# Moving four tiles of the second modulation from the second feed-forward's second down projection to the first mixer's output projection

## The reference, cut to what matters

```python
# first block, second half
x = x + mod[:, 1, 2][:, None, :] * y                 # y = ... einsum('bsd,de->bse', merged, w_out)
h = modulate(x, norm_w[l, 2], mod[:, 2, 0], mod[:, 2, 1])
x = x + 0.5 * mod[:, 2, 2][:, None, :] * swiglu(h, ffn_w13[l, 1], ffn_w2[l, 1])
# second block: modulation vectors, independent of x
mod = (jax.nn.silu(c) @ ada_w[i] + ada_b[i])[:, None, :]              # ada_w: 1024 x 6144
mod_c = (jax.nn.silu(c_ctx) @ ada_w[i][:, :n_ctx_mod] + ada_b[i][:n_ctx_mod])[None, None, :]
```

## Time and profile before

| | |
|---|---|
| median of 3 runs | 1704.6 us (1704.57 to 1707.57) |
| the profiled execution | 1707.38 us, its span 1705.6 us |
| PE busy | 1681.9 us, 99% of the span |
| DVE busy | 1145.5 us, 67% |
| ACT busy | 690.2 us, 40% |
| POOL busy | 67.4 us, 4% |
| transfers | 218.59 MB, mean 128 GB/s |
| mean granted clock of TensorE | 0.997 |

### The profile page before, as it was taken

One profiled execution on the slowest core, in us unless ns is written; L12 is line 12 of the kernel. 1 busy time (PEld: TensorE's weight loads), 2 busy tenths in 40 slices (PEclk: granted clock), 3 DMA queues, 4 the chain that ended last, 5 costly groups with the idle time before them and its releaser, 6 DMA issues.

```text
span 1705.6 us, 24579 instructions
## 1 busy us (share of the span) xinstructions
PE 1681.9 (99%) x8956; PEld 1408.0 (83%) x8956; DVE 1145.5 (67%) x2122; ACT 690.2 (40%) x1048; POOL 67.4 (4%) x56
## 2 busy tenths in 40 slices
PE   7999999999999999999999999999999999999998
PEld 5788888888878868897888888888868988989897
DVE  3778578655655686469969973469675558656563
ACT  4421222234236573354222334342466443626262
POOL 0000000011000000200000000200000200000002
PEclk9999999999999999999999999999999999999999
DMA  9866567332523302537666642354200232434231
GB/s 330 259 203 197 178 201 212 108 103 54 145 74 98 99 1 75 171 106 219 188 205 188 175 116 80 112 169 113 87 1 15 86 112 74 119 85 124 85 108 50
DMA packets 355674, 218.59 MB, mean 128 GB/s; under 512 B 8544, under 2 KB 353668, under 8 KB 355588
## 3 DMA queue, kind: packets, MB, share of 16 engines
q1 hardware_dynamic: 355356, 217.37, 43.8%
q10 hardware_dynamic: 232, 0.09, 0.0%
HBM read 215.34 MB, written 2.11 MB: 127 GB/s over the span
## 4 chain that ended last, share of the span: by engine, by line
PE 95%; DVE 2%; DMA 1%; issue 1%; ACT 0%; SPq 0%; POOL 0%; DVEq 0%; ACTq 0%; POOLq 0%
PE bank L777 24%; PE bank L779 24%; PE bank L778 24%; PE bank L1314 2%; PE bank L1315 2%; PE bank L1313 2%; PE bank L1039 2%; PE bank L1023 1%; PE bank L955 1%; PE bank L959 1%; PE bank L956 1%; PE bank L1101 1%; PE bank L1273 1%; PE bank L1075 1%; DMA GBUF<-in_w_ada 1%
## 5 line engine op out<-in xcount | busy, mean ns | idle before, releaser
L1471 ACT ACTIVATE W_HI<-RAW 128x1024 fp32r<-128x1024 f32 x278 | 292.3, 1056 | 463.2 <-PE bank L779 401.5
L777 PE MATMUL bank<-H_HI,W_HI 128*128 128x512 f32 x1090 | 426.1, 391 | 3.9 <-DVE W_LO L1955 3.8
L778 PE MATMUL bank<-H_LO,W_HI 128*128 128x512 f32 x1090 | 424.7, 390 | 0.0
L779 PE MATMUL bank<-H_HI,W_LO 128*128 128x512 f32 x1090 | 424.7, 390 | 0.0
L1955 DVE TENSOR_TENSOR W_LO<-RAW,W_HI 128x1024 fp32r<-128x1024 f32 x254 | 311.3, 1226 | 95.3 <-ACT W_HI L1471 92.1
L777 PE MATMUL bank<-A_HI,W_HI 128*128 128x512 f32 x714 | 279.7, 392 | 0.0
L778 PE MATMUL bank<-A_LO,W_HI 128*128 128x512 f32 x714 | 278.2, 390 | 0.0
L779 PE MATMUL bank<-A_HI,W_LO 128*128 128x512 f32 x714 | 278.2, 390 | 0.0
L777 PEld LDWEIGHTS bank<-H_HI,W_HI 128*128 128x128 f32 x1090 | 204.7, 188 | 49.3 <-issue 5.1
L779 PEld LDWEIGHTS bank<-H_HI,W_LO 128*128 128x128 f32 x1090 | 204.7, 188 | 42.4
L778 PEld LDWEIGHTS bank<-H_LO,W_HI 128*128 128x128 f32 x1090 | 204.8, 188 | 42.2 <-issue 0.2
(11 more groups left out here) (435 smaller groups left out, 2313.5 us busy)
## 6 DMA issues: line engine op xcount, KB each, us to landing
RAW<-in_ffn_w SPq DMA_DIRECT2D x116, 512.0 KB, 4.8
GBUF<-in_w_ada SPq DMA_DIRECT2D x32, 1024.0 KB, 7.4
RAW<-in_mlp_w SPq DMA_DIRECT2D x64, 512.0 KB, 4.1
RAW<-in_w_in SPq DMA_DIRECT2D x57, 512.0 KB, 3.9
GBUF<-in_ada_w SPq DMA_DIRECT2D x24, 1024.0 KB, 7.2
RAW<-in_w_out SPq DMA_DIRECT2D x16, 512.0 KB, 4.0
RAW<-in_ffn_w SPq DMA_DIRECT2D x16, 384.0 KB, 3.4
PBUF<-in_w_ada SPq DMA_DIRECT2D x4, 1024.0 KB, 10.9
```

Of the source, the lines that this page charges most:

```text
L777: pe.matmul(dst, w_hi, x_hi, start=first and i == 0, stop=False)
L778: pe.matmul(dst, w_hi, x_lo, start=False, stop=False)
L779: mm = pe.matmul(dst, w_lo, x_hi, start=False, stop=last and i == len(blocks) - 1)
L1471: act.activation(strip_of(W_HI, slot), strip_of(RAW, slot), ACT.Copy).then_inc(hi_ready, 1)
```

## The change

Four tiles leave the second down projection of the second feed-forward. They are now loaded between the seventh and the eighth strip of the output projection's weights, and summed behind the strips 0, 2, 3 and 4 of that projection (`GEM_OUT`), the first of them before the update of strip 0.

```diff
-                    [(8, gem_up1(0), 4, gem_down1(0)), (8, gem_up1(1), 4, gem_down1(1)), (0, None, 0, None)]]
+                    [(8, gem_up1(0), 4, gem_down1(0)), (8, gem_up1(1), 0, None), (0, None, 0, None)]]
+        GEM_OUT = (0, 2, 3, 4)
...
-            load_strips(U_OUT, KC, lambda m: w_out[:, :, bass.ds(m * P, P)])
-
-            sp.wait_ge(mlo_ready, KC)
+            for m in range(KC):
+                load_strip(U_OUT + m, (U_OUT + m) % RING, w_out[:, :, m * P:(m + 1) * P])
+                if m == KC - 2:
+                    sp.wait_ge(mlo_ready, KC)
+                    for g in range(GEM_RING):
+                        load_gem_after(g, T_ADA + g, ada2(gem_down1(1)(0, g)))
+
             sp.dma_start(CTOK[:, :].rearrange("p (t d) -> p t d", t=2),
                          a["ctx_2"][0].rearrange("(t p) d -> p t d", p=P)).then_inc(ctx_in, 16)
-            load_ffn(U_FFN1, 1, T_ADA, w13[1], w2[1], ada2)
+            load_ffn(U_FFN1, 1, T_ADA + GEM_RING, w13[1], w2[1], ada2)
...
                 def turn(it, strips):
                     for j in strips:
                         split_next(u0, it, j)
+                        if u0 == U_OUT and j == 0:
+                            gem_step(0, seq_no, vec, tile(0, 0))
                         dve.wait_ge(strip_done, it * RING + (u0 + j + 1 + RING))
...
-                        if j in gem_at:
+                        if j in gem_at and (u0 != U_OUT or j):
                             g = gem_at.index(j)
                             gem_step(g, seq_no + g, vec, tile(0, g))
...
-                down(U_OUT, MOD, 40, halves=True)
+                down(U_OUT, MOD, 40, T_ADA, C_2, gem_down1(1), GEM_OUT, halves=True)
...
-            ffn(U_FFN1, 1, T_ADA, C_2, 2 * KC, C_CTX, [last_gate, context_rms, second_modulation], [nothing, context, nothing])
+            ffn(U_FFN1, 1, T_ADA + GEM_RING, C_2, 2 * KC, C_CTX, [last_gate, context_rms, second_modulation], [nothing, context, nothing])
```

## The result

The changed kernel takes 1712.78 us in the median of 6 runs (1712.34 to 1715.07), beside 1704.59 us for the kernel before in 6 runs on the same chip: 8.2 us slower, ratio 1.0046 with a 95% interval of 1.0036 to 1.0056. A second series of five gave 1714.51 beside 1704.61, ratio 1.0048 (1.0035 to 1.0062). The forecast was 1711.8, range 1706.3 to 1715.0. The change adds 5 lines ahead of the DVE and PE code, and more inside it, so L1955 of before is L1960 here, L2130 is L2137, L912 is L917.

What follows compares the result with a forecast made beforehand. PE, busy for 99% of the span, was taken to bound the kernel. The terms −0.35 (removal), +5.5 (late norm) and +2.0 (clock) gave +7.15 us on the 1704.6 median, about 1711.8, range 1706.3 to 1715.

Steps and rivals of the forecast that it cites:

- The removal: Second down projection: four tiles of about 4.3 us of DVE time leave; PE gets back 0.35 us, nothing more.
- the two signs at 1001 and 1003 us: Expected in the changed kernel's trace: PE's two weight-load waits at the context, 0.35 and 0.22 us, are gone.
- The first tile: Ahead of the output projection's first update: summed by 704.2, X needed at 704.92; 0 lost, bounds 0 and 3.9 us.
- Tiles two to four: Behind updates of strips 2, 3 and 4 of the output projection: DVE late, PE's norm sum starts 5.5 us later.
- the two bounds of the port: In each tile, POOL's sum enters between steps, costing DVE about 1.1 us, or waits for the transpose, costing almost nothing.
- The clock: At the norm, PE's 5.5 us stop makes its clock fall to half; cost 2.0 us, bounds 0 and 3.5.
- (a): At the tiles, POOL waits for the transpose: PE 2.5 us late, 1706.7, or 1708.7 if the clock falls; 20%.
- (b): At the norm, the port costs nothing beyond what it did: 1.3 − 0.35 us, giving 1705.6; 8%.
- (d): The norm has more slack than read and the tiles hide wholly: 1704.3, no change; 5%.
- (c): Output projection: first tile lands later than 700.6, moving everything from 704.92 by up to 3.9 us more: 1712 to 1716; 7%.
- (e): Second down projection: late operands secretly slow PE's matmuls; each of eight strips gains, faster from 1.1 us per strip; 5%.
- The sum: Whole kernel: −0.35 + 5.5 + 2.0 = +7.15 us, giving a span of 1712.8 and a median of about 1711.8.

## Why the prediction was right, point by point

- **The removal: −0.35 us forecast, −0.2 measured.** That DVE's 17 us there are worth nothing was right, and the run without the tiles shows it directly. The term was mis-sized at the earlier trace rows: the 0.35 us at the fold were named a wait for DVE, but stay when DVE has long been done. From the fold's load to the next matmuls' load it was 2.1 us before and 1.9 after. So one of the two signs at 1001 and 1003 us came and the other did not.
- **The first tile: 0, as forecast.** It was there at 698.15, 1.7 us earlier than the median of the earlier trace rows gave, and the slack behind it was 2.66 us. The first update started at 705.20, past the 705 that I had set as a sign of being wrong, but 0.28 of that is the later start of the whole stretch, and DVE was waiting for PE there.
- **Tiles two to four: 5.5 us forecast, 5.28 measured.** Last split's end 735.5 forecast, 735.58 measured; POOL's last sum 736.65 and 736.70; PE's sum 736.75 and 736.80, less the 0.28 by which the stretch began later. The choice between the two bounds of the port was the step that decided: POOL got in between two instructions in all three tiles, ahead of the first step in the second tile and of the second step in the third and fourth. Its price was 1.03 us each, forecast 1.1, and the runs without POOL's sums and with PSUM sums both show it. The rule of the Trainium skill that the prediction quotes, that whoever issues first keeps the pair for its whole instruction, stands in that section under DVE's modes that use both ports; the prediction carried it over to instructions with two SBUF inputs, and the step of 1.52 us that ends 0.28 us behind POOL's sum agrees with that.
- **The clock: 2.0 us forecast, 2.23 in the profiled execution, 2.9 between medians.** The term was too small, within its bounds of 0 to 3.5, and it came that near partly by luck. The prediction took six slow microseconds, 3 us, and let 1 us of them be hidden behind ACT and DVE. In the trace the clock was down before PE resumed, and PE worked at 0.50 only from 736.80 to about 741.4 (0.78 in the mean of 741 to 742): 4.6 us, which at half speed lose 2.3. The stretch lost 2.1 to 2.2 (6.26 us beside 4.12 and 4.03), so hardly anything was hidden. The two errors nearly cancel. That PE has nothing else to do in this norm is not so either: the products of the second half fill it, and in the kernel before PE is busy in every microsecond from 731 to 735. But they stand behind the sum in PE's program, so a late sum still moves everything.
- **The rivals.** (a), POOL waiting until the transpose, is refuted by the step of 1.52 us. (b) and (d), 1.3 us or nothing lost, by the wait of 5.12. (c) did not come. (e), a hidden gain in the second down projection, is refuted by the run without the tiles.
- **The sum.** The profiled execution's span was forecast at 1712.8 and is 1713.3; the median was forecast at 1711.8 and is 1712.8. Of the 0.5 us missing in the span, 0.28 is the later start of the stretch, 0.23 the clock's term and 0.15 the removal's, less 0.22 by which the delay was forecast too large. Of the 1.0 missing in the median the rest is in the executions without the fall near the start, for which no profile of the change was taken.

What stays open: why the clock's fall costs 2.2 us in the profiled execution but more between medians (the last section shows that its price moves with the moment of the fall), and what sets, from one execution to the next, whether it falls for a wait of 1.5 to 2 us.

## What to carry to other kernels

An engine that is idle on average has no room where its last instruction of a stage releases the bottleneck: add up its work from the last point where it waits to that instruction, and compare with the idle time in between. Here three tiles were hidden at no cost that these runs can tell, and the fourth cost about 8 us. When DVE work moves to a place where POOL is active, price the meetings too: a short DVE step that reads two operands from SBUF lost 1.03 us to a POOL sum of 1.32, a long split 0.44, and a step with one operand in PSUM nothing. And if TensorE must wait anyway, a few dummy matmuls sized below the wait kept the clock up here: 22 calls gave 2.2 to 2.9 us back, 40 lost all of it to their own tail.

## What the runs showed that I had not expected

- After a wait of PE of 1.5 to 2.0 us the clock was down to 1.2 GHz in the profiled executions of three kernels, and other executions of the same kernels were 1.4 to 1.9 us faster. Of the eleven with POOL's three sums left out, six lie in the upper group by their times, the profiled one among them, whose clock is seen to fall. After a wait of 0.52 us it stayed at 1.00 in the profiled execution.
- The price of a fall depends on where it begins beside the wait's end. Where the clock stayed up, the stretch from the sum to the first matmul of the up projection took 4.0 to 4.1 us. In the change, where the clock was down at 735, 1.8 us before PE resumed, it took 6.26. In the three kernels with waits of 1.5 to 2.0 us it took 5.7: there the clock was low for about 3.4 us of PE's work. With the sums in PSUM it took 739.39 − 732.12 = 7.27 us: the clock was at 0.81 in the microsecond in which PE resumed and low for the 6.8 us behind it. So the price was 1.6, 2.2 and 3.2 us for 3.4, 4.6 and 6.8 us of PE's work at the low clock, each time a little less than half. The rows with the sums in PSUM:

```profile
730.00:732.00 2.00, 0.00 (x0) 0.00 (x0) 1.29 (x2) 1.80 (x4) 1.92 (x1) 1.00 0.77 183
732.00:733.00 1.00, 0.88 (x7) 0.89 (x7) 0.00 (x0) 0.00 (x0) 0.01 (x1) 0.81 0.79 241
733.00:734.00 1.00, 1.00 (x6) 1.00 (x7) 0.11 (x1) 0.26 (x1) 0.00 (x0) 0.50 1.09 376
...
738.00:739.00 1.00, 1.00 (x7) 1.00 (x6) 1.00 (x4) 0.63 (x2) 0.00 (x0) 0.50 0.13 30
```

- Two single-operand products (L1986) took 0.98 us instead of 0.61 while POOL's second sum still ran, though they read only one tile from SBUF. That is the 0.4 us that the forecast had set there. Written into PSUM, the same two products took 0.86 us beside that sum (at 707.16) and 0.87 with POOL quiet (at 713.93), so nothing was lost to POOL there. Which port they need is not shown by any run.
